# Expert gate and up weights loaded two blocks side by side in 2 MB transfers, and the last six down pieces of five visits multiplied in fp32

## What is computed

```python
# per expert e, for the tokens that the router sends to it
y_e = (silu(x @ moe_w_gate[0, e]) * (x @ moe_w_up[0, e])) @ moe_w_down[0, e]
y = y + combine[:, e:e + 1] * y_e
x = layer_norm(ALPHA * x + y, ln2_g[1], ln2_b[1])
```

## Time and profile before

| | |
|---|---|
| median of 3 runs | 1504.56 us (1502.7 to 1506.28) |
| span of the profiled execution | 1504.0 us |
| mean granted TensorE clock | 0.981 of full speed |
| busy share | TensorE 94%, VectorE 89%, ScalarE 74%, GpSimd 7% |
| DMA | 464.86 MB in 141347 packets, mean 309 GB/s |
| first load of expert weights issued | 575.8 us |

### The profile page before, as it was taken

One profiled execution on the slowest core, in us unless ns is written; L12 is line 12 of the kernel. 1 busy time (PEld: TensorE's weight loads), 2 busy tenths in 40 slices (PEclk: granted clock), 3 DMA queues, 4 the chain that ended last, 5 costly groups with the idle time before them and its releaser, 6 DMA issues.

```text
span 1504.0 us, 40039 instructions
## 1 busy us (share of the span) xinstructions
PE 1418.1 (94%) x17659; PEld 1161.2 (77%) x17659; DVE 1331.8 (89%) x1324; ACT 1107.7 (74%) x1036; POOL 111.0 (7%) x160
## 2 busy tenths in 40 slices
PE   7999999999999999899999999999999889898786
PEld 5888878888888788698687797788777776766663
DVE  4999987545569899899999999999999999999997
ACT  4797755444358676587897878888888888978884
POOL 2121014000043001200000000000000000000001
PEclk8999999999999999999999999999999999999898
DMA  9654466457554527879999999999999999999993
GB/s 316 237 168 155 162 235 219 141 183 236 171 180 141 172 87 270 345 304 380 405 413 392 412 411 397 411 409 394 411 407 410 412 406 411 411 401 410 411 396 132
DMA packets 141347, 464.86 MB, mean 309 GB/s; under 512 B 8234, under 2 KB 10410, under 8 KB 126800
## 3 DMA queue, kind: packets, MB, share of 16 engines
q1 hardware_dynamic: 138960, 457.21, 79.7%
q0 software_dynamic: 1920, 4.55, 1.0%
q10 hardware_dynamic: 288, 0.48, 0.1%
HBM read 460.79 MB, written 2.89 MB: 308 GB/s over the span
## 4 chain that ended last, share of the span: by engine, by line
PE 56%; DVE 29%; DMA 5%; issue 4%; ACT 3%; POOL 1%; SPq 1%; DVEq 0%; ACTq 0%
PE ps L859 17%; PE ps L860 17%; PE ps L861 17%; DVE w_lo L2274 13%; DVE w_lo L2277 6%; ACT w_hi L1655 2%; PE ps L972 2%; DMA x<-in_moe_w_gate 2%; DMA stage<-in_w_in 2%; DMA stage<-in_moe_w_up 1%; DVE w_lo L1746 1%; POOL x L786 1%; DVE arena L2292 1%; DVE arena L2312 1%; SPq L646 1%
## 5 line engine op out<-in xcount | busy, mean ns | idle before, releaser
L861 PE MATMUL ps<-arena,w_lo 128*128 128x128 f16 (+7 forms) x3952 | 568.9, 215 | 13.7 <-issue 13.6
L859 PE MATMUL ps<-arena,w_hi 128*128 128x128 f16 (+7 forms) x3952 | 569.1, 215 | 13.4 <-issue 6.6
L860 PE MATMUL ps<-arena,w_hi 128*128 128x128 f16 (+7 forms) x3952 | 569.1, 215 | 11.3 <-issue 11.3
L859 PEld LDWEIGHTS ps<-arena,w_hi 128*128 128x128 f16 x3952 | 388.3, 100 | 28.9 <-issue 16.9
L860 PEld LDWEIGHTS ps<-arena,w_hi 128*128 128x128 f16 x3952 | 388.2, 100 | 25.1 <-issue 16.5
L861 PEld LDWEIGHTS ps<-arena,w_lo 128*128 128x128 f16 x3952 | 388.2, 100 | 12.8 <-issue 6.9
L859 PE MATMUL ps<-xhl,w_hi 128*128 128x264 f16 x1120 | 312.0, 279 | 11.8 <-DVE w_lo L1746 4.6
L860 PE MATMUL ps<-xhl,w_hi 128*128 128x264 f16 x1120 | 311.9, 278 | 0.0
L861 PE MATMUL ps<-xhl,w_lo 128*128 128x264 f16 x1120 | 311.8, 278 | 0.0
L1746 DVE SCALAR_TENSOR_TENSOR w_lo<-stage,w_hi 128x2048 f16<-128x2048 f32 (+1 forms) x95 | 210.5, 2236 | 81.7 <-ACT w_hi L1352 81.4
L1352 ACT ACTIVATE w_hi<-stage 128x2048 f16<-128x2048 f32 (+1 forms) x95 | 174.5, 1853 | 88.1 <-PE ps L861 75.3
(11 more groups left out here) (345 smaller groups left out, 1937.1 us busy)
## 6 DMA issues: line engine op xcount, KB each, us to landing
stage<-in_moe_w_up SPq DMA_DIRECT2D x57, 1024.0 KB, 14.0
stage<-in_moe_w_down SPq DMA_DIRECT2D x56, 1024.0 KB, 14.4
stage<-in_w_in SPq DMA_DIRECT2D x43, 1024.0 KB, 5.5
mixer_only<-in_moe_w_up SPq DMA_DIRECT2D x39, 1024.0 KB, 13.1
stage<-in_moe_w_gate SPq DMA_DIRECT2D x33, 1024.0 KB, 8.4
arena<-in_moe_w_gate SPq DMA_DIRECT2D x32, 1024.0 KB, 13.4
mixer_only<-in_moe_w_gate SPq DMA_DIRECT2D x24, 1024.0 KB, 13.7
x<-in_moe_w_down SPq DMA_DIRECT2D x16, 1024.0 KB, 14.8
```

The costliest lines, as they stand in the source:

```text
L859: mm(out, ah, bh, start=start, stop=False, skip_group_check=True)
L860: mm(out, ah, bl, start=False, stop=False, skip_group_check=True)
L861: return mm(out, al, bh, start=False, stop=stop, skip_group_check=True)
```

## The change

The loads: gate and up of blocks 0 and 1 (2048 columns) are loaded together, in four loads of 256 rows, 2 MB each; those of blocks 2 and 3 (1536 columns) in four loads of 1.5 MB; down goes in seven loads of 2 MB. A visit has 23 loads where it had 42. The row of a gate or up load is 8 KB or 6 KB long where it was 4 KB (2 KB for block 3). There are seven homes of 2 MB. A load waits until the last piece that uses the home's former load is split (`LAST_OF`), or, for a piece that isn't split, used by TensorE (`piece_used`).

The order of pieces: gate 0 and 1 in turn, up 0 and 1 in turn, gate 2 and 3 in turn, down 0 and 1, up 2 and 3, down 2 and 3. Pieces are still 1 MB, 42 a visit, with six slots. A piece now lies in its home as two or four separate row segments, and `lo_of` splits it with one VectorE instruction for each segment. ScalarE's `hi_of` has one for each load.

The fp32 pieces: in visits 1, 4, 5, 6 and 7 (`FP32_DOWN`) the last six pieces, down of blocks 2 and 3, are neither split nor copied; TensorE multiplies them in fp32 out of their homes, with the hidden values in fp32.

```diff
-RING = 14
-TWICE = 5
+BIG = 2 * PIECE
+HOMES_AFTER = [2, 3, 4, 0, 1, 5, 6]
...
+ORDER = visit_order()
+VISIT = len(ORDER)
+LOADS = ([("g", 0, q) for q in range(4)] + [("u", 0, q) for q in range(4)] + [("g", 1, q) for q in range(4)]
+         + [("d", 0, c) for c in range(4)] + [("u", 1, q) for q in range(4)] + [("d", 0, c) for c in range(4, NC)])
+LAST_OF = [max(m for m in range(VISIT) if j in loads_of(m)) for j in range(NLOADS)]
+FP32_DOWN = (1, 4, 5, 6, 7)
+FP32_FROM = ORDER.index(("d", 2, 0))
+NSPLIT = [FP32_FROM if v in FP32_DOWN else VISIT for v in range(NE)]
...
+            def load_used(at, j):
+                m = LAST_OF[j]
+                if m < NSPLIT[at[1]]:
+                    sp.wait_ge(S["lo_done"], split_so_far(at, m + 1))
+                else:
+                    sp.wait_ge(*piece_used(at, m))
...
+                        if as_landed_:
+                            t = mm(ps[0:cap, b, :], h[:, cols], rows[:, k * D + half * 512:k * D + half * 512 + 512],
+                                   start=start, stop=stop, skip_group_check=True)
...
+            def lo_of(at, m):
+
+                parts = list(zip(halves_of(at, m, w_lo), halves_of(at, m, w_hi)))
+                for (src, dst), (_, hi) in parts[:-1]:
+                    V.scalar_tensor_tensor(dst, src, WS, hi, ALU.mult, ALU.subtract)
+                (src, dst), (_, hi) = parts[-1]
+                V.scalar_tensor_tensor(dst, src, WS, hi, ALU.mult, ALU.subtract).then_inc(S["lo_done"], 1)
...
+                    if m == 33:
+                        hidden(at, 2, silu_e, silu_e)
+                    if m == 34 and split_all:
+                        hidden_lo(at, 2, silu_e)
+                    if m == 35:
+                        hidden(at, 3, h_fp32[:, 3:4, :], h_fp32[:, 3:4, :])
+                    if m == 36 and split_all:
+                        hidden_lo(at, 3, h_fp32[:, 3:4, :])
+                    if m + SLOTS < NSPLIT[v]:
+                        lo_v(at, m + SLOTS)
+                    elif m + SLOTS >= VISIT and v < NE - 1:
+                        lo_v((at[0], v + 1), m + SLOTS - VISIT)
```

More of the change, by code:

```diff
@@ L514, in paired, with landed, home_of @@
[L514 to L520, removed]
+        def home(n):
+            return stage[:, n % SLOTS, :]
+        def landed(n):
+            return stage_full[n % SLOTS], 16 * (n // SLOTS + 1)
+        def home_of(i, first):
+            return i if first and i < 2 else HOMES_AFTER[(i - 2) % len(HOMES)]
+        HOME_LOADS = [[sum(home_of(i, first) == h for i in range(NE * NLOADS)) for h in range(len(HOMES))]
+                      for first in (True, False)]
@@ new lines, in load_landed, with load_home @@
+        def load_landed(at, j):
+            r, v = at
+            i = v * NLOADS + j
+            first = isinstance(r, int) and r == 0
+            h = home_of(i, first)
+            turn = sum(home_of(k, first) == h for k in range(i))
+            if first:
+                return home_full[h], 16 * (turn + 1)
+            return home_full[h], r * (16 * HOME_LOADS[1][h]) + 16 * (HOME_LOADS[0][h] - HOME_LOADS[1][h] + turn + 1)
+        def load_home(at, j):
+            return HOMES[home_of(at[1] * NLOADS + j, isinstance(at[0], int) and at[0] == 0)]
@@ new lines, in split_so_far, with blocks_split, piece_used @@
+        def split_so_far(at, n):
+            r, v = at
+            return r * sum(NSPLIT) + (split(PRE) + sum(NSPLIT[0:v]) + n)
+        def blocks_split(at, n):
+            r, v = at
+            return r * sum(HSPLIT) + (1 + sum(HSPLIT[0:v]) + n)
+        def piece_used(at, m):
+            r, v = at
+            kind, b, q = order[m]
+            if m in part_in_visit:
+                return S["part_used"], so_far((r, v), NPART, PART0 + part_in_visit.index(m) + 1)
+            if kind == "d":
+                return in_visit(bank_full, 5, at, 2)
+            return in_visit(bank_full, GU_BANKS[kind, b][-1], at, GU_FILL[kind, b])
@@ L634, in trunk_kernel @@
         NPROD = CW - 2
-        GATHER_AT = VISIT - 2
         block = ctx.enter_context(nc.Block())
@@ L659, in _, with visits @@
                 load(*pre_piece(n), n)
-            def visits(r, first=False):
+            def visits(r):
+                first = isinstance(r, int)
                 for v in range(NE):
@@ L2322, in token_norms, with next_round @@
+            def next_round(r):
+                for m in range(SLOTS):
+                    lo_v((r, 0), m)
             def token_norms(nv):
```

542 lines of the change are left out of this document (288 added, 254 removed).

## The result

The changed kernel takes 1537.82 us in the median (1537.12 to 1538.68) against 1504.9 us before: a ratio of 1.0216, 95% interval 1.0201 to 1.0230. The forecast was 1513.5 with a range up to 1530. The sign was right, and the size was off by a factor of almost four. The profiled execution spans 1536.7 us, 32.7 more than the earlier trace rows. One execution of the later run a_bank ran at a granted clock of 0.556 (span 2467.1); its profile isn't used, and its ratio leaves that one out.

What follows compares the result with a forecast made beforehand. DMA, VectorE and TensorE were all nearly full, VectorE bounding visits 1 and 4 to 7, TensorE visit 2. Chain +4.2 and stream +10.5 were rival readings; the later, less overlap, gave +9, plus 0.6: 1513.5 us, range 1498 to 1530.

Steps and rivals of the forecast that it cites:

- the order that comes with it: In fp32 visits, VectorE's splits to piece 35 and then TensorE's fp32 pieces become a chain; said to decide.
- The fp32 chain: Visits 1 and 3 to 7: VectorE's splits, piece 35, gather, then 20.7 us of fp32 on TensorE; sum +4.2 us.
- Small instructions: VectorE's cut gate and up splits: 1024 elements start 1.14 us apart, costing 2.9 us a visit; upper end 5.9.
- The stream: Weight loads: 1.1% faster, 411.6 GB/s over all, but homes freed later; last landing 1479, end +10.5 us.
- Its lead: Loads landed ahead by visit 1's start at 750.6 us: 53 of 336 pieces, where it was 56.
- what I had taken off for overlap: At the end: +10.5 us lowered to +9 because the stream's stops overlap VectorE's waits.
- The tail: From the last weight landing to TensorE's last expert matmul: 18.2 us, where it was 9.6.
- Visit 4 over 107: Sign expected in the middle of the kernel: visit 4 takes over 107 us; the chain had 110.0.
- VectorE under 95% in visits 4 to 7: Sign expected in visits 4 to 7: VectorE busy less than 95% of the time.
- A gap before block 3's product: Sign expected on VectorE in visits 4 to 7: a gap before each product of block 3; no size given.
- the faster rival: Expert part: the stream alone counts, ending at 1498 us, decided by a last landing under 1468; chance 0.18.
- DMA under 9 tenths near 720: Sign expected near 720 us, before visit 1: DMA share falls below 9 tenths.

Runs made afterwards that it cites:

- a_bank: a_first with TensorE's wait for PSUM bank 2 ahead of visit 0's first gate matmul taken away; 1526.16 us, ratio 1.0137.
- m_only: o_only with up 2 put ahead of down 1 again (1 MB loads, no fp32 piece); 1515.42 us, ratio 1.0067.
- m_best: m_gather without the bank 2 wait ahead of visit 0, and with the last visit's second residual rows behind piece 39; 1504.15 us, ratio 0.9996.
- m_gather: m_only with the gather of the next visit's tokens behind TensorE's piece 39, not 35, and ScalarE's copy ahead of step 40; 1515.42 us, ratio 1.0060.
- o_fp32: Changed kernel with its loads undone (1 MB loads, 14 homes, uncut splits), new order and fp32 down pieces kept; 1522.23 us, ratio 1.0108.
- m_fp32: m_only with the six down pieces of visits 1 and 4 to 7 in fp32; 1520.90 us, ratio 1.0096.
- a_first: Changed kernel with ScalarE taking the first expert piece's high part behind the mixer's merged tiles, not ahead of them; 1531.92 us, ratio 1.0179.
- o_only: Changed kernel with its loads undone (1 MB loads, 14 homes, uncut splits) and no fp32 piece, leaving the new order alone; 1524.96 us, ratio 1.0126.
- a_fp16: Changed kernel with no down piece in fp32, all 42 pieces of every visit split; 1547.21 us, ratio 1.0285.
- a_mech: a_first with up 2 ahead of down 1 in pieces and loads, the changed kernel's big loads kept; 1571.0 us, ratio 1.0439.
- a_whole: Whole pieces split again in one VectorE instruction under the new loads; gave no time, as the instruction takes two free dimensions and needs three.

## Why the prediction was wrong, point by point

The runs give a sum for the 32.9: order +19.8, fp32 pieces -2.7, cut splits +7.7, loads and homes +7.9, together 32.7. The differences were taken in this order, and in another they come out otherwise: the fp32 pieces are -9.4 if taken last.

**The order cost 19.8 and was priced at nothing.** This is the step that failed. The forecast wrote of "the order that comes with it" only in the fp32 visits, and began with visit 1 at 750.6. It had no term for what TensorE waits for at the seams, where one visit or stage passes to the next. The runs show three such waits: block 2's hidden values needed right behind up 2 and 3 (9.5 by m_only), bank 2 ahead of visit 0 (5.8 by a_bank), and the residual rows' bank behind silu of gate 3 (about 5.6 by m_best's trace).

Two things limit this division. m_best also holds m_gather's edit, the gather behind piece 39; without the other two it changed no time, but it made visits 1 to 6 shorter by 7.5, so a fourth wait, at the gather, may stand in these numbers. And with the fp32 pieces in, as the changed kernel has them, the first of the three is worth 1.3 (o_fp32 to m_fp32), not 9.5.

What two runs show in the changed kernel itself is the part ahead of visit 1. The forecast had it at 750.6 and it began at 762.0, 11.4 later. Taking away ScalarE's wait at the first load (a_first, 5.9) and TensorE's at bank 2 (a_bank, 5.8) gives back 11.7, nearly half of the 24.3 by which the forecast missed.

**The fp32 chain exists, but it was too short.** The forecast's chain was +3.6 in visit 1, +5.6 in visits 3 and 4, -0.2, -2.5 and -2.3 in visits 5 to 7, sum +4.2. The changed kernel against the kernel before has +5.9, +10.6, +1.4, -0.2 and +3.3 (visit 7 to TensorE's last expert matmul), sum +21.0; visit 2 adds 0.3, and with the 11.4 ahead of visit 1 that is the 32.7.

Under the repaired order and old loads, m_fp32 against m_only has +3.4, +4.6, -1.2, -1.9, +1.3, sum +6.2. That this is near the forecast's +4.2 is luck in part. The forecast had the cut splits in its chain (68.4 us for 30 splits), and m_fp32 has none (30 x 2.20 = 66.0). Less 2.4 a visit, its visits 1, 5, 6 and 7 would be 103.2, 100.3, 99.8 and 99.2, my estimate from its own terms; m_fp32's are 106.7, 104.2, 103.0 and 104.2.

In the changed kernel the fp32 pieces pay (-9.4). VectorE has 2.2 more to do in each visit there and idles at the seams, so that 13 us less of splits may outweigh the chain; this is argued from the traces.

**Small instructions: right in the spacing, and below the lower bound in the sum.** VectorE's 1024-element halves start 1.14 apart (1271.48, 1272.62, 1273.76, in the changed kernel's visit 5), not 1.22. The forecast 2.9 a visit measured 2.2, and 7.7 to 7.9 in all, since only four visits pay it. The Trainium skill's 58-cycle figure ("VectorE: DVE Perf Modes", the TRN2 errata), 2.2 by my estimate, agrees with the 2.2; the 150-cycle one doesn't.

**The stream.** Its rate was about right: in clean windows 417 and 421 GB/s, for 413 and 415 forecast. Its lead was not. The forecast had 53 pieces landed at 750.6; 42 and three loads of two, 48, had. One of the five is arithmetic: 24.6 us at 2.55 a piece are 9.6 pieces, not 10 to 11. (The mean of the old rates is 409.5, not 410.1, which changes little.) The first load of visit 1 went at 731.1 (forecast 724), and visit 0 itself had begun 8.3 late. Between visits 0 and 1 nothing lands for 11.1 us (729.2 to 740.3), where a 2 MB load takes 5. Last landing 1499.8 for 1479: that is 20.8 of the 24.3 us by which I missed; 1.5 are the tail, 1.5 what I had taken off for overlap, and the rest is the median over the span, 1.1 for 0.6.

**The tail** was forecast at 18.2 and is 19.7, but the fp32 pieces are not what made it long. Without any it is 24.8 in o_only and 29.5 in a_fp16, and 10.6 in m_best. So this number came out near for another reason than the forecast gave: the order made the tail long, and the fp32 pieces shortened it.

**The signs I named.** Visit 4 over 107: yes, 109.85. VectorE under 95% in visits 4 to 7: yes, 75 to 89%. A gap before block 3's product: yes, 3.03 in visit 5. The last fp32 matmuls: 48 records in 20.74 us, 0.43 each, as forecast. Next visits' first loads some 28 us before the visit's end: yes, 28 to 31. Fp32 visits under 100 us or a landing before 1468 (the faster rival): no. DMA under 9 tenths near 720: yes, 0.81 in visit 0 (320 GB/s), but it was 0.91 (356) before, too: the forecast read 9 tenths in every slice from 650 us on, and the earlier trace rows has 7 in the slice from 639 to 677. I had read this as a stop in passing; it was carried to the end.

What stays open: the three waits add to 20.9 where o_only has 19.8, with intervals of some 2 us each, and the gather wasn't tested apart in the mended order. No run has the order of before with the fp32 pieces, so what the order costs beside them isn't measured whole. Why the fp32 pieces give 9.4 under the new loads and 2.7 under the old was read from the traces only. a_bank has no usable trace, so its 5.8 goes by medians alone.

## What to carry to other kernels

A change of layout that forces a new order of work is first a change of order: list for each seam what the first instruction behind it waits for (bank, token copy, hidden values), in the first and the last stage too, before pricing instructions. Here that part was 19.8 of 32.9 us, taken first, and two of the three waits were no part of the idea and could be taken away in a few lines. Measure such a part with the rest of the change in place, too: the remaining wait was worth 9.5 us without the fp32 pieces and 1.3 with them.

In a kernel where the loads, VectorE and TensorE are all nearly full, a wait of 3 to 5 us ahead of the steady part came back whole at the end, and more (a_first: a wait of 4.8, 5.9 in the median; a_bank: 3.35 and 5.8). The bigger loads gained 1 to 2% of rate (410 to 418 GB/s in visits 4 to 6, for 407 to 409) and held each home longer; one that joins pieces used far apart stopped the stream (a_mech, 39 us).

## Not expected of the hardware

Nothing in the runs was strange for the chip. VectorE's three-operand instruction could be given at most two free dimensions (a_whole), where ScalarE's activation has three (it writes `w_hi` in one instruction for each load), so a layout can cost one engine and not the other.
